# Attention: key copies, rotary exchange and score order

## The chip, the cores and the metric

The kernel runs on one core of a Trainium2 chip. The metric is device time in microseconds, the median of several executions.

## The reference

One inference step of a denoising trunk of four layers. A layer is a half-step SwiGLU feed-forward, a mixer, and a second such feed-forward, each with RMS norms around it and with shift, scale and gate from a conditioning vector; that makes twelve sub-layers. The mixers are attention (layers 0 and 3), a short convolution and a bidirectional gated scan. There are 128 prompt tokens and 256 sample tokens of 1024 features, in fp32. The attention has 16 query heads and 4 key/value heads of 64 features. For the sample tokens, queries and keys are rotated, and the keys are those of the band of 128 positions around the query and 128 cached ones; for the prompt tokens there is no rotation:

```python
def apply_rope(x, cos, sin):
    x1, x2 = jnp.split(x, 2, axis=-1)
    return jnp.concatenate([x1 * c - x2 * s, x1 * s + x2 * c], axis=-1)
s_lat = einsum(q, k_band) * ATTN_SCALE          # masked to the window
s_ctx = einsum(q, k_ctx) * ATTN_SCALE
p = softmax(concatenate([s_lat, s_ctx, sink]))
o = p_lat @ v_band + p_ctx @ v_ctx ;  return o.reshape(B, L, ATTN_DIM) @ w_o
```

The outputs are the tokens of both groups, the prompt's keys and values, and the scan's states.

## The kernel before, in words

All 384 tokens are kept together, features across the 128 partitions. Each weight block of 128 x 1024 comes by one load into one of four raw buffers; ScalarE rounds it to a high part (line 1925) and VectorE subtracts for the low part (line 2081), in a ring of six; three products of high and low parts make one product of TensorE (lines 1671 to 1673, 24 passes per block). There is no scheduler: each engine has its own list of work, written out by hand, and waits on semaphores. SyncE issues the loads in block order; load b waits until block b - 4 is split (`need(sp, w_lo_made, b - RAW + 1)`).

The attention is sub-layers 1 and 10. It has twelve projection blocks of 128 features, in the order of `QKV_CHUNKS`: two of keys, query 0, two of values, queries 1 to 7, and then eight blocks of the output weight. A query block holds two heads. Its parts:

- `take` (line 713, ScalarE) copies a projection out of PSUM. `dup` (line 568) is a product with a 0/1 matrix that puts one key head on both halves of the partitions; `copy_key` (line 728) takes it out to `kd`.
- `rotate` (line 580) is a product with a permutation that exchanges the 32-feature halves of the sample tokens of one key head or query block. GpSimd multiplies the original by the cosine (`cosine`, line 885), VectorE the exchanged one by the sine out of PSUM (line 803), and adds them (line 807). There are twelve rotations per attention, five of them ahead of the loop.
- `scores` (lines 595 to 603) are the products of a query block with keys and cached keys, `maxima` (line 819), `probs` (line 746) and `normalize` (lines 834 to 840) the softmax; `turn_probs` (line 614) transposes a head's probabilities, `values` (lines 632 to 639) multiplies them with the values, `output` (lines 753 and 754) copies the result and GpSimd's `low_part` (line 889) makes its low part.
- The loop has seven steps j. In each TensorE projects one block (step j: block 5 + j, query j + 1), transposes head 2j - 2, rotates the new query, does `values(j - 2)`, transposes head 2j - 1 and does `scores(j + 1)`. In step 0 it transposes the values and the prompt's keys instead (line 555).
- In sub-layer 1 alone a unit of the modulation is computed inside the attention, out of eight slabs of 512 KB (line 1792; `unit_half`, four slabs each), loaded by SyncE among the weights: three at b = 3, three at b = 6, two at b = 8 (`load_unit`).

Of the kernel before, what the change touches and what calls it, by code (L numbers as in the profile page):

```python
# [14 lines left out]
P = 128  # L15
D = 1024
# [29 lines left out]
def host_constants():  # L46
# [7 lines left out]
    rot = np.zeros((P, P), np.float32)  # L54
    rot[m ^ 32, m] = 1.0
    dup = np.zeros((P, 2, P), np.float32)
    duprot = np.zeros((P, 2, P), np.float32)
    for g in range(2):
        dup[64 * g + m % 64, g, m] = 1.0
        duprot[64 * g + ((m % 64) ^ 32), g, m] = 1.0  # L60
# [11 lines left out]
    attn = np.concatenate([rot, dup.reshape(P, -1), duprot.reshape(P, -1), cos, sin * sign,  # L72
                           band[:, 0].reshape(P, -1), np.zeros((P, P)), band[:, 1].reshape(P, -1)],
# [20 lines left out]
def build(nc, ins, outs, n_sub=12):  # L94
# [35 lines left out]
    QKV_CHUNKS = [DC, DC + 1, 0, DC + 2, DC + 3] + list(range(1, DC))  # L130
# [208 lines left out]

    def stores_until(s):  # L340

        return 2 * sub_kind[:s].count("attn")
# [33 lines left out]
    attn_k = place("attn_k", [P, 5 * P + 2 * TS + KEYS], F32, x_end - 2 * D * 4)  # L376
# [14 lines left out]
    rot_m = attn_k[:, 0:P]  # L391
    dup_m = [attn_k[:, P * (1 + g):P * (2 + g)] for g in range(2)]
    duprot_m = [attn_k[:, P * (3 + g):P * (4 + g)] for g in range(2)]
    cos_t = attn_k[:, 5 * P:5 * P + TS]
    sin_t = attn_k[:, 5 * P + TS:5 * P + 2 * TS]
    band_t = attn_k[:, 5 * P + 2 * TS:]
# [3 lines left out]
    rope_rot, k_dup_done, k_dup_copied = sem("rope_rot"), sem("k_dup_done"), sem("k_dup_copied")  # L400
# [118 lines left out]
    ROPE_ORDER = [("k", 0), ("k", 1), ("q", 0), ("k", 2), ("k", 3)] + [("q", j) for j in range(1, DC)]  # L519
    FIRST_ROPES = 5  # L520
    Q_AT = {j: ROPE_ORDER.index(("q", j)) for j in range(DC)}

    def qkv_bank(p):

        return p if p < 4 else 0 if p == 4 else 7

    def rope_bank(n):

        return 6 + n % 2 if n < FIRST_ROPES else 7

    def rope_dst(n):
        kind, i = ROPE_ORDER[n]
        return kd[:, i, TP:T] if kind == "k" else qkv[:, i, TP:T]

    def pe_attn(pe, s, first_two, in_block, out_part, ada_half, ada_turn):
        mm = nc.tensor.matmul
        a, mi, b0 = attn_number(s), mixer_number(s), first_block[s]
        taken = len(QKV_CHUNKS) * a
# [8 lines left out]
        def turn_values():  # L547

            pe.wait_ge(qkv_taken, taken + 5)
            pe.wait_ge(k_dup_copied, KVH * (a + 1))  # L550
            for n in range(NT + 1):
                for c in range(2):
                    src = qkv[:, DC + 2 + c, n * P:(n + 1) * P] if n < NT else qkv[:, DC + c, 0:P]
                    at = 2 * (n % 2) + c
                    last = nc.tensor.transpose(psum[4 + n // 2][:, at * P:(at + 1) * P], src, ident)
                if n % 2 == 1:
                    last.then_inc(attn_turned, 1)

        def dup(g):

            if g == 0:
                pe.wait_ge(qkv_taken, taken + 1)
            elif g == 1:
                pe.wait_ge(attn_turn_copied, 4 * a + 1)
            else:
                pe.wait_ge(qkv_taken, taken + 2)
                pe.wait_ge(k_dup_copied, KVH * a + g - 1)
            mm(psum[4 + (g + 1) % 2][:, 0:T], dup_m[g % 2], qkv[:, DC + g // 2, :], start=True,
               stop=True).then_inc(k_dup_done, 1)

        def rotate(n):
            kind, i = ROPE_ORDER[n]
            if n >= FIRST_ROPES:
                pe.wait_ge(qkv_taken, taken + n + 1)
            elif n >= 2:
                pe.wait_ge(rope_sin, ROPE * a + n - 1)
                if kind == "q":
                    pe.wait_ge(qkv_taken, taken + 3)
# [296 lines left out]
    def gp_attn(gp, s):  # L875
# [18 lines left out]
        for n in range(FIRST_ROPES):  # L894
            cosine(n)
# [1558 lines left out]
```

## Time and profile before

| | |
|---|---|
| time, median of 3 runs (lowest, highest) | 3026.55 us (3024.98, 3030.62) |
| profiled execution: span from the first to the last instruction | 3023.0 us |
| TensorE busy | 2968.9 us, 98% |
| VectorE, ScalarE, GpSimd busy | 73%, 38%, 20% |
| first attention, scores 0 to the first output product | 354.52 to 428.01 us |
| mean granted TensorE clock | 0.997 |

The profiled execution's own time is its span and what lies around it; no other time of it is kept, so it is set beside the median of the runs. The profile is one execution. Times in a timeline are microseconds from the start of the span. PE is TensorE, DVE VectorE, ACT ScalarE, POOL GpSimd, SPq SyncE's queue. A plain fp32 product shows as two passes. Durations of TensorE's passes overlap, so what a group holds is read from the start of its first pass to the start of the work behind it.

### The profile page before, as it was taken

The page shows a single profiled execution, that of the slowest core. Times are in us where ns is not written, and L with a number is a line of the kernel's source. Part 1 is how long each engine was busy: PE and PEld are TensorE (multiplying, and loading weights), DVE is VectorE, ACT ScalarE, POOL GpSimd, SP SyncE. Part 2 cuts the span into 40 slices and gives each one's busy share as a digit, 9 for nine tenths or more (in the row PEclk, how much of TensorE's full clock was granted, in tenths as well). Part 3 has the DMA queues.
Part 4 walks back from the last instruction along what each step waited for, and adds up shares of the span by engine and source line. Part 5 has one row for each costly group of instructions (what it writes and reads, how often), then busy time and mean ns, then how long its engine had stood idle before and what let it go on. Part 6 is the DMA issues. An engine that isn't in the chain of part 4 may idle for free.

```text
span 3023.0 us, 46915 instructions
## 1 busy us (share of the span) xinstructions
PE 2968.9 (98%) x18458; PEld 2750.8 (91%) x18458; DVE 2194.7 (73%) x2831; ACT 1152.8 (38%) x1966; POOL 594.5 (20%) x586
## 2 busy tenths in 40 slices
PE   7999999999999999999999999999999999999999
PEld 6999888999999998999899999979999999888998
DVE  6888678887877656888887576768887888775444
ACT  4222664223322424222422365553224222664222
POOL 1111212112211212112211144541122112211001
PEclk9999999999999999999999999999999999999999
DMA  8667435665665445766566443337675766333443
GB/s 303 208 212 215 138 86 190 209 209 168 212 210 172 117 134 166 222 211 197 181 209 202 133 117 95 103 96 230 209 215 166 222 211 197 110 79 119 126 127 96
DMA packets 565935, 515.61 MB, mean 171 GB/s; under 512 B 43013, under 2 KB 499286, under 8 KB 563926
## 3 DMA queue, kind: packets, MB, share of 16 engines
q1 hardware_dynamic: 565158, 512.37, 55.7%
q8 instruction: 148, 2.42, 0.3%
q14 instruction: 69, 0.57, 0.1%
q10 hardware_dynamic: 560, 0.25, 0.0%
HBM read 509.31 MB, written 3.24 MB: 170 GB/s over the span
## 4 chain that ended last, share of the span: by engine, by line
PE 91%; issue 3%; DVE 2%; ACT 1%; POOL 1%; DMA 1%; SPq 0%; DVEq 0%; POOLq 0%; ACTq 0%
PE bank L1671 19%; PE bank L1673 19%; PE bank L1672 19%; PE bank L1720 9%; PE bank L1722 9%; PE bank L1721 9%; PE bank L1688 2%; PE bank L1695 1%; PE bank L614 1%; PE bank L639 1%; PE bank L1753 1%; DMA ada_first<-w_ada 1%; POOL small L2358 0%; POOL small L2363 0%; ACT tmp L1978 0%
## 5 line engine op out<-in xcount | busy, mean ns | idle before, releaser
L1671 PE MATMUL bank<-h_hi,w_hi 128*128 128x384 f32 x3328 | 1120.7, 337 | 0.0
L1673 PE MATMUL bank<-h_hi,w_lo 128*128 128x384 f32 x3328 | 1115.1, 335 | 0.0
L1672 PE MATMUL bank<-h_lo,w_hi 128*128 128x384 f32 x3328 | 1114.0, 335 | 0.0
L1925 ACT ACTIVATE w_hi<-raw 128x1024 fp32r<-128x1024 f32 x646 | 680.5, 1061 | 1030.9 <-PE bank L1673 478.2
L2081 DVE TENSOR_TENSOR w_lo<-raw,w_hi 128x1024 fp32r<-128x1024 f32 x648 | 812.2, 1277 | 328.5 <-ACT w_hi L1925 323.6
L2108 DVE SCALAR_TENSOR_TENSOR fold<-ada_raw,cond,fold 128x1024 f32<-128x1024 f32 x462 | 638.7, 1439 | 0.1
L1671 PEld LDWEIGHTS bank<-h_hi,w_hi 128*128 128x128 f32 x3328 | 625.5, 188 | 10.9 <-ACT tmp L1944 1.6
L1672 PEld LDWEIGHTS bank<-h_lo,w_hi 128*128 128x128 f32 x3328 | 625.4, 188 | 6.1
L1673 PEld LDWEIGHTS bank<-h_hi,w_lo 128*128 128x128 f32 x3328 | 625.3, 188 | 0.0
L2399 POOL TENSOR_TENSOR h_lo<-tmp,h_hi 128x384 fp32r<-128x384 f32 x176 | 280.4, 1593 | 1737.6 <-DVE h_hi L2142 1737.6
L1720 PE MATMUL bank<-w_hi,h_hi 128*128 128x512 f32 x1056 | 415.4, 393 | 0.0
L1722 PE MATMUL bank<-w_hi,h_lo 128*128 128x512 f32 x1056 | 413.7, 392 | 0.0
L1721 PE MATMUL bank<-w_lo,h_hi 128*128 128x512 f32 x1056 | 413.2, 391 | 0.0
L1944 ACT ACTIVATE tmp<-bank 128x384 f32<-128x384 f32 x176 | 86.5, 491 | 481.4 <-PE bank L1673 479.1
L2138 DVE TENSOR_TENSOR tmp<-bank,tmp 128x384 f32<-128x384 f32 x176 | 97.9, 556 | 230.7 <-PE bank L1673 228.5
L1722 PEld LDWEIGHTS bank<-w_hi,h_lo 128*128 128x128 f32 x1056 | 198.2, 188 | 42.2
L1720 PEld LDWEIGHTS bank<-w_hi,h_hi 128*128 128x128 f32 x1056 | 198.3, 188 | 38.4
L1721 PEld LDWEIGHTS bank<-w_lo,h_hi 128*128 128x128 f32 x1056 | 198.3, 188 | 37.9
L2002 ACT ACTIVATE hf<-bank,mod,s_cols 128x128 f32<-128x128 f32 x288 | 106.5, 466 | 33.9 <-PE bank L1753 27.4
L2180 DVE TENSOR_TENSOR og<-bank,g_rows 128x512 f32<-128x512 f32 x72 | 49.3, 685 | 53.0 <-ACT tmp L1978 53.0
L1720 PE MATMUL bank<-w_hi,o_hi 128*128 128x512 f32 x192 | 77.1, 401 | 1.4 <-DVE tmp L942 1.0
L2115 DVE TRANSPOSE_TENSOR_REDUCE fold_sums<-fold 128x64 f32<-128x2048 f32 x33 | 76.0, 2304 | 0.0
(204 smaller groups left out, 2422.4 us busy)
## 6 DMA issues: line engine op xcount, KB each, us to landing
raw<-w_ffn_in SPq DMA_DIRECT2D x352, 512.0 KB, 5.0
ada_raw<-w_ada SPq DMA_DIRECT2D x264, 512.0 KB, 4.2
raw<-w_ffn_out SPq DMA_DIRECT2D x176, 512.0 KB, 4.6
raw<-w_hgrn_in SPq DMA_DIRECT2D x40, 512.0 KB, 4.0
g_rows<-g_dram SPq DMA_DIRECT2D x12, 1024.0 KB, 6.7
raw<-w_attn_qkv SPq DMA_DIRECT2D x24, 512.0 KB, 6.1
raw<-w_conv_in SPq DMA_DIRECT2D x24, 512.0 KB, 4.9
ada_first<-w_ada SPq DMA_DIRECT2D x16, 512.0 KB, 11.7
```

Of the source, the lines that this page charges most:

```text
L1671: mm(out, wh, h_hi[:, k, :], start=(k == 0), stop=False)
L1672: mm(out, wh, h_lo[:, k, :], start=False, stop=False)
L1673: last = mm(out, wl, h_hi[:, k, :], start=False, stop=(k == DC - 1))
L1720: mm(out, hi[:, tokens(t)], w_hi[:, b % RING, columns(n)], start=opens, stop=False)
L1721: mm(out, hi[:, tokens(t)], w_lo[:, b % RING, columns(n)], start=False, stop=False)
L1722: return mm(out, lo[:, tokens(t)], w_hi[:, b % RING, columns(n)], start=False, stop=closes)
L1925: A(w_hi[:, b % RING, :], raw[:, b % RAW, :], ACT.Copy).then_inc(w_hi_made, 1)
L2002: last = A(hf[:, t, k, :], psum[2 * t + half][:, k % 4 * P:(k % 4 + 1) * P], ACT.Identity, bias=mod[:, 3 * e * DC + k, g:g + 1], scale=s_c ...
L2081: V.tensor_tensor(w_lo[:, b % RING, :], raw[:, b % RAW, :], w_hi[:, b % RING, :].bitcast(F32), ALU.subtract).then_inc(w_lo_made, 1)
L2108: V.scalar_tensor_tensor(out=acc, in0=slab, scalar=c, in1=acc, op0=ALU.mult, op1=ALU.add).then_inc(fold_made, 1)
L2138: V.tensor_tensor(tmp[:, 2 + f % 2, :], psum[7][:, 0:T], tmp[:, f % 2, :], ALU.mult).then_inc(b_read, 1)
L2399: G.tensor_tensor(h2_lo[:, f % H2, :], tmp[:, 2 + f % 2, :], h2_hi[:, f % H2, :].bitcast(F32), ALU.subtract).then_inc(h2_lo_made, 1)
```

## The change

The products `dup` and `rotate` are gone, with their constant matrices. The two key projections are copied out of PSUM twice each, to both halves of the partitions, by ScalarE (first) and VectorE (second). The halves are exchanged by transfers within SBUF that SyncE issues, two for a key head and four for a query block, into four buffers; GpSimd then does both products and the sum. The last value block is projected last, so each query is projected a step earlier; its values are transposed in step 6. In steps 1 and 6 `scores(j + 1)` stand ahead of `values` and the second transpose. On SyncE the key exchanges 0, 1 and 3 stand ahead of load 8, exchange 5 ahead of load 13, the others behind a load (`KEY_SWAPS`, `QUERY_SWAPS`).

```diff
-    QKV_CHUNKS = [DC, DC + 1, 0, DC + 2, DC + 3] + list(range(1, DC))
+    QKV_CHUNKS = [DC, DC + 1, 0, DC + 2] + list(range(1, DC)) + [DC + 3]
...
-    attn_k = place("attn_k", [P, 5 * P + 2 * TS + KEYS], F32, x_end - 2 * D * 4)
+    attn_k = place("attn_k", [P, 2 * TS + KEYS], F32, x_end - 2 * D * 4)
...
+    rope_more = place("rope_more", [P, 2, TS], F32, x_end - 2 * TS * 4)
+    rope_of = [rope_tmp[:, 0, :], rope_tmp[:, 1, :], rope_more[:, 0, :], rope_more[:, 1, :]]
+    ROPE_BUFFERS = len(rope_of)
...
-    ROPE_ORDER = [("k", 0), ("k", 1), ("q", 0), ("k", 2), ("k", 3)] + [("q", j) for j in range(1, DC)]
-    FIRST_ROPES = 5
+    TAKES = len(QKV_CHUNKS) - 2
+    FIRST_BLOCKS = 5
+    ROPE_ORDER = [("k", 0), ("k", 1), ("q", 0), ("k", 2), ("q", 1), ("k", 3)] + [("q", j) for j in range(2, DC)]
+    FIRST_ROPES = 6
+    KEY_SWAPS, QUERY_SWAPS = {8: (0, 1, 3), 13: (5,)}, {8: 2, 13: 4} | {b: b - 8 for b in range(14, 20)}
...
+    def swap_runs(n):
+        if ROPE_ORDER[n][0] == "k":
+            return [(0, 32, 96), (96, 0, 32)]
+        return [(to, to ^ 32, 32) for to in range(0, P, 32)]
...
+    def copy_keys(copy, c):
+        rows = [slice(0, HD), slice(HD, P)]
+        copy(qkv[:, DC + c, 0:TP], psum[c][:, 0:TP])
+        for x in range(2):
+            for half in rows:
+                last = copy(kd[half, 2 * c + x, :], psum[c][rows[x], 0:T])
+        return last
...
-            pe.wait_ge(rope_sin, ROPE * a + FIRST_ROPES + j - (1 if j == 0 else 0))
-            in_block(b0 + FIRST_ROPES + j, 7)
+            pe.wait_ge(qkv_taken, taken + take_number(FIRST_BLOCKS + j - 1))
+            in_block(b0 + FIRST_BLOCKS + j, 7)
             if j == 0:
                 turn_values()
             else:
                 turn_probs(2 * j - 2)
-            rotate(FIRST_ROPES + j)
+            if j in (1, DC - 2):
+                if j == DC - 2:
+                    turn_last_values()
+                scores(j + 1)
             if j >= 2:
                 values(j - 2)
             if j >= 1:
                 turn_probs(2 * j - 1)
-            scores(j + 1)
+            if j not in (1, DC - 2):
+                scores(j + 1)
...
-        def cosine(n):
+        def rope(n):
+            gp.wait_ge(rope_swapped[n % ROPE_BUFFERS], swaps_made(a, n))
+            G.tensor_tensor(rope_of[n % ROPE_BUFFERS], rope_of[n % ROPE_BUFFERS], sin_t, ALU.mult).then_inc(rope_sin, 1)
+            G.tensor_tensor(rope_place(n), rope_place(n), cos_t, ALU.mult).then_inc(rope_cos, 1)
+            gp.wait_ge(rope_sin, ROPE * a + n + 1)
+            gp.wait_ge(rope_cos, ROPE * a + n + 1)
+            G.tensor_tensor(rope_place(n), rope_place(n), rope_of[n % ROPE_BUFFERS], ALU.add).then_inc(rope_add, 1)
...
+        def swap(s, n):
+            a, (kind, i) = attn_number(s), ROPE_ORDER[n]
+            if kind == "k":
+                sp.wait_ge(k_copied[i // 2], a + 1)
+            else:
+                sp.wait_ge(qkv_taken, TAKES * a + take_number(QKV_CHUNKS.index(i)))
+            need(sp, rope_add, ROPE * a + n + 1 - ROPE_BUFFERS)
+            for to, of, rows in swap_runs(n):
+                sp.dma_start(rope_of[n % ROPE_BUFFERS][to:to + rows, :], rope_place(n)[of:of + rows, :]
+                             ).then_inc(rope_swapped[n % ROPE_BUFFERS], 16)
...
             for b in range(n_blocks(s)):
+                if sub_kind[s] == "attn":
+                    for n in KEY_SWAPS.get(b, ()):
+                        swap(s, n)
                 if s > 0 or b >= 4:
                     load_block(b0 + b)
+                if sub_kind[s] == "attn" and b in QUERY_SWAPS:
+                    swap(s, QUERY_SWAPS[b])
```

## Rows read from the trace of the kernel before

**Rows 1.** Page, part 4: the chain that ended last, by engine.
```profile
PE 91%; issue 3%; DVE 2%; ACT 1%; POOL 1%; DMA 1%; SPq 0%; DVEq 0%; POOLq 0%; ACTq 0%
```

**Rows 2.** Windows, one loop step: us, busy by engine, clock, DMA share, GB/s.
```profile
372.36:382.35 9.99, 9.99 (x89) 9.03 (x88) 8.91 (x29) 7.58 (x23) 0.73 (x1) 1.00 0.18 54
```

**Rows 3.** Timeline, TensorE, first attention ahead of its loop: start, us, instruction.
```profile
336.76 0.81 PE L568 MATMUL bank<-qkv,attn_k 128*128 128x384 f32 x2
338.37 0.42 PE L1792 MATMUL bank<-unit_slab,cond 128*32 128x256 f32 x4
...
344.52 0.81 PE L568 MATMUL bank<-qkv,attn_k 128*128 128x384 f32 x2
346.77 1.93 PE L1792 MATMUL bank<-unit_slab,cond 128*32 128x256 f32 x32
...
353.27 0.89 PE L568 MATMUL bank<-qkv,attn_k 128*128 128x384 f32 x2
354.52 0.49 PE L595 MATMUL bank<-kd,qkv 64*128 64x256 f32 x2
```

**Rows 4.** Timeline, TensorE, first attention: in the loop.
```profile
361.41 0.60 PE L580 MATMUL bank<-qkv,attn_k 128*128 128x256 f32 x2
363.41 0.49 PE L595 MATMUL bank<-kd,qkv 64*128 64x256 f32 x2 [1.40 <-DVE qkv L807]
...
370.20 0.68 PE L580 MATMUL bank<-qkv,attn_k 128*128 128x256 f32 x2
371.48 0.30 PE L614 MATMUL bank<-base_k,pr 128*128 128x128 f32 x1 [0.60 <-ACT pt L737]
...
379.15 0.68 PE L580 MATMUL bank<-qkv,attn_k 128*128 128x256 f32 x2
379.76 0.33 PE L632 MATMUL bank<-pt,vt 128*64 128x128 f32 x2
```

**Rows 5.** Timeline, TensorE, second attention: before the loop.
```profile
2617.24 0.81 PE L568 MATMUL bank<-qkv,attn_k 128*128 128x384 f32 x2
2619.20 0.52 PE L1671 MATMUL bank<-h_hi,w_hi 128*128 128x384 f32 x1
...
2624.72 0.49 PE L595 MATMUL bank<-kd,qkv 64*128 64x256 f32 x2
```

**Rows 6.** Tile view, the unit's last slab: issue ns, when, landing.
```profile
L1572 SPq DMA_DIRECT2D unit_slab<-w_ada x1: 433/433/433, 340.7 to 340.7; - x1
DMA to landing us min/median/max: 4.9/4.9/4.9
```

**Rows 7.** Timeline, ScalarE: copy of query 0 in the first and second attention.
```profile
342.43 0.47 ACT L713 ACTIVATE qkv<-bank 128x384 f32<-128x384 f32 x1
...
2614.09 0.47 ACT L713 ACTIVATE qkv<-bank 128x384 f32<-128x384 f32 x1
```

**Rows 8.** Groups by line, GpSimd's cosine product: count, busy us, mean ns.
```profile
L885 POOL TENSOR_TENSOR qkv<-qkv,attn_k 128x256 f32<-128x256 f32 x16 | 11.7, 732 | 93.1 <-PE bank L580 93.1
```

**Rows 9.** DMA view, issues by line: KB each, median us to landing.
```profile
hg_in<-state_hgrn SPq DMA_DIRECT2D x8, 128.0 KB, 3.6
```

**Rows 10.** Waits of SyncE's queue, 280 to 440: total us, times, longest.
```profile
SPq L1582 <- DMA g_dram<-g_out: 8.4, 1, 8.4
```

**Rows 11.** Timeline, VectorE and GpSimd: two instructions that overlap.
```profile
382.93 1.00 DVE L834 TENSOR_TENSOR soft<-soft 128x3 f32<-128x3 f32 x1
...
382.91 1.00 POOL L889 TENSOR_TENSOR o_lo<-tmp,o_hi 128x384 fp32r<-128x384 f32 x1 [2.27 <-ACT o_hi L754]
```

**Rows 12.** Windows of 1 us, 324 to 328: first and last of four.
```profile
324.00:325.00 1.00, 1.00 (x6) 1.00 (x6) 0.53 (x2) 1.00 (x5) 1.00 (x2) 0.60 0.00 0
...
327.00:328.00 1.00, 1.00 (x8) 1.00 (x8) 1.00 (x2) 1.00 (x2) 1.00 (x1) 0.69 0.00 0
```

**Rows 13.** Timeline, VectorE: the weight split in step 0, first attention.
```profile
363.27 1.22 DVE L2081 TENSOR_TENSOR w_lo<-raw,w_hi 128x1024 fp32r<-128x1024 f32 x1
```

**Rows 14.** Page, part 5, ScalarE's weight split: count, busy us, mean ns.
```profile
L1925 ACT ACTIVATE w_hi<-raw 128x1024 fp32r<-128x1024 f32 x646 | 680.5, 1061 | 1030.9 <-PE bank L1673 478.2
```

More of the change, by code:

```diff
@@ L338, in build, with tokens @@
     out_stored = sem("out_stored")
+    def tokens(t):
+        return slice(t * P, (t + 1) * P)
     def stores_until(s):
@@ L537, in pe_attn @@
         a, mi, b0 = attn_number(s), mixer_number(s), first_block[s]
-        taken = len(QKV_CHUNKS) * a
+        taken = TAKES * a
         def turn_cache():
@@ L547, in turn_values @@
         def turn_values():
[L549 to L578, printed above, removed]
-            stat, src = (duprot_m[i % 2], DC + i // 2) if kind == "k" else (rot_m, i)
-            mm(psum[rope_bank(n)][:, 0:TS], stat, qkv[:, src, TP:T], start=True, stop=True).then_inc(rope_rot, 1)
+            pe.wait_ge(qkv_taken, taken + take_number(3))
@@ new lines, in turn_values, with turn_last_values @@
+            for c in range(2):
+                pe.wait_ge(k_copied[c], a + 1)
+            pe.wait_ge(attn_turn_copied, 4 * a + 1)
+            for n in range(NT):
+                nc.tensor.transpose(psum[5][:, tokens(n)], qkv[:, DC + 2, tokens(n)], ident)
+            for c in range(2):
+                last = nc.tensor.transpose(psum[4][:, c * P:(c + 1) * P], qkv[:, DC + c, 0:TP], ident)
+            last.then_inc(attn_turned, 1)
+        def turn_last_values():
+            pe.wait_ge(qkv_taken, taken + TAKES)
+            for n in range(NT):
+                last = nc.tensor.transpose(psum[7][:, tokens(n)], qkv[:, DC + 3, tokens(n)], ident)
+            last.then_inc(attn_turned, 1)
@@ L582, in scores @@
         def scores(j):
             g = 2 * j // (HEADS // KVH)
-            pe.wait_ge(rope_add, ROPE * a + Q_AT[j] + 1)
-            pe.wait_ge(k_dup_copied, KVH * a + g + 1)
+            pe.wait_ge(rope_add, ROPE * a + max(ROPE_AT["q", j], ROPE_AT["k", g]) + 1)
             if j == 0:
-                pe.wait_ge(qkv_taken, taken + 5)
+                for c in range(2):
+                    pe.wait_ge(k_copied[c], a + 1)
+                pe.wait_ge(qkv_taken, taken + take_number(3))
             else:
@@ L648, in unit_half @@
             if half == 0:
-                pe.wait_ge(qkv_taken, taken + 2)
+                pe.wait_ge(k_copied[1], a + 1)
             else:
@@ L657, in pe_attn @@
         turn_cache()
-        dup(0)
-        pe.wait_ge(qkv_taken, taken + 1)
-        rotate(0)
-        rotate(1)
         for u in units:
@@ L774, in act_attn @@
             probs(2 * j)
-            take(FIRST_ROPES + j)
+            take(FIRST_BLOCKS + j)
             if j == 0:
@@ L779, in act_attn @@
                 copy_probs(2 * j - 2)
+            if j == DC - 2:
+                copy_last_values()
             probs(2 * j + 1)
@@ L1525, in group_of @@
         return 0 if t == 0 else 1
-    def tokens(t):
-        return slice(t * P, (t + 1) * P)
     def square_number(e, t, n, of_y):
```

92 lines of the change are left out of this document (28 added, 64 removed).

## The prediction

> **What bounds the kernel now.** First the chain of waits: TensorE holds 91% of it, so a microsecond taken from TensorE's own queue is a microsecond of the time, unless something else then comes late [rows 1]. Then busy time by stretch: in a middle step of the attention loop TensorE is busy for 9.99 of 9.99 us, VectorE for 8.91, ScalarE for 7.58, GpSimd for 0.73 [rows 2]. VectorE is the next limit, and GpSimd has room. Then TensorE's timeline, for what the rotary products cost where they stand [rows 3 to 5]. Other sub-layers aren't touched.
>
> The sum is made against the profiled execution: its span is 3023.0 us, and the median of the runs shown, 3026.55, lies 3.55 above it. I add that again at the end.
>
> **What goes.** Per attention, four products that double the keys and twelve that exchange halves.
> - Ahead of the loop, in the first attention: from the first product to the next other work 1.61, 2.25 and 1.25 us, 5.11 in all [rows 3]. In the second the middle group takes 1.96 for 2.25 [rows 5]; with the others in that ratio it is 4.45.
> - In the loop: step 0, the product and the wait for the rotated query, 363.41 - 361.41 = 2.00. Step 1, the product and 0.60 of waiting for ScalarE, 371.48 - 370.20 = 1.28. Steps 2 to 6, 379.76 - 379.15 = 0.61 each, 3.05. Together 6.33 [rows 4].
> - The transposes are eight as before; three of them (some 0.33 us) go from step 0 to step 6.
> The ceiling is 5.11 + 4.45 + 2 x 6.33 = 22.2 us. On VectorE, two rotary instructions per step go; at step 0 they held 363.27 - 361.41 = 1.86 us with their waits [rows 13].
>
> **What comes, at its price.** A query's exchange is four issues on SyncE, one after the other. I take 0.43 each, from a slab's issue [rows 6]: the last starts 1.3 us after the first, and SyncE is held 1.7. No transfer within SBUF and none of 32 KB is in this trace. The nearest row for the landing is a state of 128 KB, 3.6 us [rows 9]. Below, it can't be less than the issue, 0.43; above, the strided 8 KB write of gains held SyncE for 8.4 [rows 10]. I take 3.6. The Trainium skill, DMA: Bandwidth & Descriptors, "Anatomy of one DMA", puts the fixed part at about 2.0 us (fitted on GpSimd's path); by it the sum would gain some 4 us more, and no row here shows it.
>
> A rotation is three GpSimd instructions of 128x256 where there was one of 0.73 [rows 8]: 2.3 us with the wait between them. Six stand ahead of the loop, one behind the other, 14 us. In the loop they stand ahead of the subtraction that makes the low part, one per step: 2.3 + 1.0 us in a step of 9.4, and ScalarE's output needs only the subtraction of two chunks before, so I cost this at nothing; were it late, ScalarE's copies would be by the same amount.
>
> The keys' copies, five on ScalarE and five on VectorE at up to 0.5 each [rows 7], lie beside TensorE's third and fourth projection: nothing. Without that cover 2.5 us once. VectorE's part also holds SyncE: the third key's exchange waits for it, and weight load 8 behind that. The smaller constants land before the stage and save nothing.
>
> **First attention.** The new wait that matters is query 0's exchange on SyncE, ahead of the last two slabs of the modulation unit. It waits for ScalarE's copy, which ends at 342.43 + 0.47 = 342.90 because it stands behind a split [rows 7]. Four issues later, at 344.6 and 345.0, come the slabs; the second was issued at 340.7 and landed 4.9 later [rows 6]. So it lands at 349.9, and with the last quarter of the unit's product (0.48) TensorE goes on at 350.4. Before, that product ended at 346.77 + 1.93 = 348.70 [rows 3]. The first two of the three groups are thus lost, and 1.7 us more. The third group's 1.25 is saved, but it covered VectorE's addition to the modulation, of which I estimate 0.35 exposed (it lies between 0 and 1.25). Scores 0 start at 354.52 + 1.7 - 0.9 = 355.3: 0.8 late.
> - Scores 1: they followed scores 0 by 363.41 - 354.52 = 8.89 [rows 3, 4]; less 2.00 and 0.33, TensorE is ready at 355.3 + 6.56 = 361.9. Query 1's projection runs some 4.3 us from 350.4, its copy ends at about 355.2; last issue 356.5, landing 360.1, rotated 362.4. Gain there: 363.4 - 362.4 = 1.0.
> - Scores 2, now ahead of a transpose: the exchange stands behind load 14, which waits for VectorE's split. That ended at 363.27 + 1.22 = 364.49, 9.97 after scores 0 began [rows 3, 13]; without the rotary part 8.1, so at 363.4. Load 0.4, last issue 1.3, landing 3.6, rotation 2.3: 371.0. TensorE is ready 370.20 - 363.41 = 6.79 after scores 1 [rows 4], at 369.2, and waits for 1.8. Scores and transpose have only changed places, and the first of the two began at 371.48 [rows 4]: gain 0.5.
> - Steps 2 to 6: the same chain takes 8.1 + 7.6 = 15.7 us from one scores to the next but one, and two steps of 9.99 - 0.61 = 9.4 leave 3 to spare; scores 7, moved up, have some 0.5. So 3.05 - 0.33 = 2.7 more.
> Net gain 3.2.
>
> **Second attention.** No unit here. Query 0's copy ends at 2614.09 + 0.47 = 2614.56 [rows 7]; last issue 2615.9, landing 2619.5, rotated 2621.8. TensorE would be ready at 2624.72 - 4.45 = 2620.3 [rows 5]: gain at scores 0 only 2.9. Load 9, now behind that exchange, is issued at 2616.3 and lands about 2620.3 (4.0, my estimate from the 3.6 and an issue); with both splits, 1.06 and 1.22 [rows 13, 14], load 13 can go at 2622.6, and behind it query 1's exchange: rotated at 2622.6 + 7.6 = 2630.2, where TensorE is ready at 2621.8 + 6.56 = 2628.4. Scores 2 by the chain: 2621.8 + 15.7 = 2637.5 (ready 2637.0). Its place before, at the first attention's distances, was 2624.72 + 371.48 - 354.52 = 2641.7: gain 4.2. With 2.7 for the steps: 6.9.
>
> Sum: 3.2 + 6.9 = 10.1 us. 3023.0 - 10.1 + 3.55 = 3016.5. Of the ceiling, 12 us come back as late exchanges.
>
> **The rivals.**
> - *All rotations in time* (the exchange lands almost with its issue): all waits but the slabs' go. First attention -0.8 + 6.33, second 4.45 + 6.33, together 16.3: 3010.2. For it: 32 KB is little. Against it: 128 KB took 3.6.
> - *GpSimd holds VectorE up, and VectorE becomes the bound.* A 128x3 addition of VectorE that started at 382.93 took 1.00 us, as long as GpSimd's 128x384 subtraction, started at 382.91 [rows 11]. If every rotation does that, VectorE has 8.91 - 0.85 + 2.2 = 10.3 per step against TensorE's 9.4; ten steps lose 0.9 each, 9 us of the 10: 3025.6. It decides once over 1.3 of a rotation's 2.2 us fall on such VectorE instructions; against it, the three maxima of each head read PSUM. The Trainium skill, SBUF — State Buffer, "Who interferes with whom", says so of any VectorE instruction with two SBUF inputs beside a GpSimd one that reads SBUF: the later one blocks fully. The rows agree.
> - *Late exchanges, slower.* If an exchange lands like the gains' write, 8.4 us, the chain from split to rotated query is 21.2 us, more than two steps, and the loop runs at 10.6 a step where it was 10.0. With the first waits 4.8 longer the first attention loses some 8 and the second 8: 3042. It decides from a landing of about 5.4. For it: only those 8.4 us. Against it: that write goes to HBM in elements, this one moves rows of 1 KB.
> - *Clock.* TensorE will stand still for some 5 us between 343 and 350. After a smaller stop the granted clock fell to 0.60 from 324 and was back in the fourth slice, 0.69 [rows 12]; such a fall costs half of some 3.5 us, 1.7: 3018.2. It is inside the forecast's own range.
> - *The products don't bound* (TensorE's queue waits elsewhere for all that is freed): nothing changes. Rows 1 and 2 speak against it.
>
> **How the numbers follow.** The forecast has 0.52, all in time 0.18, VectorE bound 0.20, late exchanges 0.07, no effect 0.03. No change means within 0.2%, 6 us, which is about what a measurement can tell here. Forecast and all in time count as faster, and 0.04 of VectorE bound: 0.74. Same: 0.13 of VectorE bound, 0.01 of the late ones, 0.03: 0.17. The rest, 0.09, is slower. The range from 3007 to 3025 takes in all in time with the clock's 1.7 and more, and nearly all of VectorE bound; what it leaves out is the late exchanges.
>
> **What would show it.** Right: no product with the constants on TensorE; a stop of TensorE until about 349.9 on the slabs in the first attention; scores 0 about 0.8 later there and 2.9 earlier in the second; waits of 0.5 to 2 us for GpSimd's addition before scores 1 and 2; middle steps of 9.4. An exchange that lands in under 2 us, or waits for GpSimd in the middle steps, would refute the sizes; VectorE splits much over 1.2 us with TensorE waiting for a normalised head would show the lock. Wrong altogether: middle steps of 10 or more.

## The result: slower by 0.4%

The changed kernel took 3038.77 us (median of 5 runs, 3035.39 to 3043.78), the kernel before 3026.55 beside it: a ratio of 1.0039, 95% interval 1.0029 to 1.005. The forecast was 3016.5 and its range ended at 3025; sign and size were both wrong. The profiled execution of the changed kernel, 3043.78 us with a span of 3042.0, was the slowest of the five; that of before, with a span of 3023.0, lies at the fast end of its runs. So the traces differ by 19.0 us and the medians by 12.2.

TensorE's share of the chain of waits fell, and every other engine's grew [rows 1]:
```profile
PE 86%; issue 4%; DVE 4%; DMA 2%; ACT 2%; POOL 2%; SPq 1%; another core or an unknown queue 0%; DVEq 0%; POOLq 0%; ACTq 0%
```

The middle step of the loop did what was foretold. Window of one step: us, then busy time (and count) of TensorE, its weight loads, VectorE, ScalarE and GpSimd, granted clock, DMA share, GB/s [rows 2]:
```profile
400.62:410.07 9.45, 9.45 (x87) 8.70 (x86) 8.88 (x27) 7.29 (x23) 3.12 (x4) 1.00 0.24 72
```
A step takes 9.45 us instead of 9.99, and TensorE is never idle. But VectorE is still busy for 8.88 (8.91 before), though two of its instructions went.

The time went where TensorE stops. Its timeline in the first attention (start, us, instruction, and in brackets the idle time before it with what ended it) [rows 3, 4]:
```profile
347.04 1.28 PE L1785 MATMUL bank<-unit_slab,cond 128*32 128x256 f32 x16 [4.41 <-ACT ada_rows L1925]
351.21 1.08 PE L1785 MATMUL bank<-unit_slab,cond 128*32 128x256 f32 x8 [2.90 <-DMA unit_slab<-w_ada]
352.57 1.08 PE L1785 MATMUL bank<-unit_slab,cond 128*32 128x256 f32 x8 [0.28 <-DMA unit_slab<-w_ada]
...
360.66 0.70 PE L598 MATMUL bank<-kd,qkv 64*128 64x256 f32 x4 [0.27 <-DVE mod L2115]
...
379.07 1.23 PE L598 MATMUL bank<-kd,qkv 64*128 64x256 f32 x4 [4.81 <-POOL qkv L864]
...
433.88 0.80 PE L598 MATMUL bank<-kd,qkv 64*128 64x256 f32 x2 [7.06 <-POOL qkv L864]
...
2643.11 0.70 PE L598 MATMUL bank<-kd,qkv 64*128 64x256 f32 x4 [2.59 <-issue]
2653.14 0.70 PE L598 MATMUL bank<-kd,qkv 64*128 64x256 f32 x4 [3.30 <-POOL qkv L864]
...
2706.99 0.70 PE L598 MATMUL bank<-kd,qkv 64*128 64x256 f32 x4 [1.06 <-POOL qkv L864]
```
The last three rows are of the second attention [rows 5]. Scores 0 start at 360.66 (354.52 before), scores 2 stop for 4.81 us and scores 7 for 7.06: the two that were moved up in their steps. From the first product of the key projection to the first product of the output, the first attention takes 122.40 us (104.06 before), the second 96.15 (97.64 before). So the first is 18.3 us longer and the second 1.5 shorter; 2 us more lie outside, where 27.0 us were at the lower clock instead of 18.0.

In the first attention the stops over 0.25 us add up to 22.6 us (2.5 before), 20.1 more. The removed products take off 9.4 (the ceiling of 5.11 + 6.33 without its 2.00 of waiting). That makes 10.7 of the 18.3. Of the other 7.6, slow products explain some 6.3, as an estimate: TensorE worked for 15.9 us at the lower clock (3.4 before), and half of the difference counts as lost. The last 1.3 stay open. Windows of 7 us, same columns as above [rows 12]:
```profile
347.00:354.00 7.00, 3.79 (x33) 1.24 (x34) 1.09 (x1) 0.36 (x1) 6.57 (x10) 0.55 0.90 265
354.00:361.00 7.00, 6.73 (x32) 6.62 (x33) 1.82 (x3) 1.97 (x3) 0.69 (x1) 0.71 1.00 291
...
434.00:441.00 7.00, 7.00 (x55) 6.17 (x55) 0.00 (x0) 0.71 (x2) 0.77 (x1) 0.58 0.02 1
```
At the three long stops of this attention the granted clock falls to its lower level, 1.2 GHz: for 10.2 us from 347.8, for 10.2 from 429.7 (4.2 of them still in the stop), and for 3.4 from 378.5, 23.9 us in this attention where before had 3.4.

Who was late is read from SyncE's issues [rows 6]:
```profile
334.81 3.55 SPq L1572 DMA_DIRECT2D rope_tmp<-kd  x4
...
339.69 0.59 SPq L1530 DMA_DIRECT2D raw<-w_attn_qkv  x1
344.64 2.42 SPq L1572 DMA_DIRECT2D rope_more<-qkv  x4
347.10 1.06 SPq L1548 DMA_DIRECT2D unit_slab<-w_ada  x2
...
370.27 0.33 SPq L1530 DMA_DIRECT2D raw<-w_attn_o  x1
370.70 2.41 SPq L1572 DMA_DIRECT2D rope_more<-qkv  x4
...
420.21 0.34 SPq L1530 DMA_DIRECT2D raw<-w_attn_o  x1
420.65 2.41 SPq L1572 DMA_DIRECT2D rope_more<-qkv  x4
423.10 0.58 SPq L1553 DMA_DIRECT2D g_dram<-g_out  x1
```
and ScalarE's copies of queries 0, 2 and 7 [rows 7]:
```profile
344.13 0.49 ACT L708 ACTIVATE qkv<-bank 128x384 f32<-128x384 f32 x1
...
366.87 0.49 ACT L708 ACTIVATE qkv<-bank 128x384 f32<-128x384 f32 x1 [0.69 <-PE bank L1666]
...
416.27 0.49 ACT L708 ACTIVATE qkv<-bank 128x384 f32<-128x384 f32 x1 [0.67 <-PE bank L1666]
```
Query 2 is in SBUF at 367.36 and its exchange is issued at 370.70; query 7 at 416.76 and 420.65. Both stand behind a weight load, and the load behind VectorE's split. VectorE's timeline shows why that split is not earlier than before [rows 13]:
```profile
366.94 1.64 DVE L822 TENSOR_SCALAR pr<-pr,soft 128x384 f32<-128x384 f32 x3
368.50 1.75 DVE L2074 TENSOR_TENSOR w_lo<-raw,w_hi 128x1024 fp32r<-128x1024 f32 x1
...
416.57 2.48 DVE L822 TENSOR_SCALAR pr<-pr,soft 128x384 f32<-128x384 f32 x3
418.97 1.21 DVE L2074 TENSOR_TENSOR w_lo<-raw,w_hi 128x1024 fp32r<-128x1024 f32 x1
...
420.97 0.95 DVE L822 TENSOR_SCALAR pr<-pr,soft 128x384 f32<-128x384 f32 x3
```
Three normalising passes take 0.95 us alone and 2.48 beside GpSimd's rotation and low part (415.58 to 418.83). The split of step 0 ends at 370.25, 9.6 us after scores 0; before it was 9.97. From query 2 on, each 32 KB issue of an exchange landed 2.4 to 3.7 us later [rows 9], but for the last one of query 7 in the first attention, which took 9.0. The keys' issues, with weights and slabs in flight, took 1.8 to 7.2 us.

### The profile page after: what moved, and what is told of

Same layout as the page of the kernel before. It is cut to its first block, busy times and chain, and to the rows that moved or that the text cites. A ratio compares the mean times of both kernels' runs of the same rounds, so it can differ in the third digit from the quotient of the medians.

```text
span 3042.0 us, 46885 instructions
## 1 busy us (share of the span) xinstructions
PE 2961.4 (97%) x18394; PEld 2747.0 (90%) x18394; DVE 2190.8 (72%) x2793; ACT 1152.1 (38%) x1964; POOL 634.9 (21%) x634
## 4 chain that ended last, share of the span: by engine, by line
PE 86%; issue 4%; DVE 4%; DMA 2%; ACT 2%; POOL 2%; SPq 1%; another core or an unknown queue 0%; DVEq 0%; POOLq 0%; ACTq 0%
PE bank L1664 18%; PE bank L1666 18%; PE bank L1665 18%; PE bank L1713 9%; PE bank L1715 9%; PE bank L1714 8%; PE bank L1681 2%; PE bank L1688 1%; DVE pr L822 1%; DMA raw<-w_attn_qkv 1%; DVE sm L801 1%; PE bank L1746 1%; DMA ada_first<-w_ada 1%; ACT pr L739 1%; DMA rope_more<-qkv 0%
```

## Experiments

Theory A: the exchanges are late, by their place in SyncE's queue, and the clock falls behind the stops. Theory B: GpSimd's operations hold VectorE up. Theory C: the moved scores ask too early. Each run was timed against the kernel before in the same session (medians 3024.95 to 3026.55). The spans of the attentions are measured as above; "half" is the time at 1.2 GHz in the first.

| kernel | median us | ratio [95%] | first attention | half | second |
|---|---|---|---|---|---|
| before | 3026.55 | 1 | 104.1 | 3.4 | 97.6 |
| changed | 3038.77 | 1.0039 [1.0029, 1.0050] | 122.4 | 23.9 | 96.2 |
| no_rotation | 3013.50 | 0.9960 [0.9946, 0.9975] | 97.9 | 0 | 89.5 |
| lock_only | 3018.29 | 0.9976 [0.9967, 0.9986] | 101.2 | 0 | 93.7 |
| no_exchange | 3019.42 | 0.9985 [0.9975, 0.9994] | 102.2 | 3.4 | 93.8 |
| no_move | 3031.80 | 1.0021 [1.0011, 1.0030] | 111.5 | 13.7 | 97.0 |
| unit_first | 3033.09 | 1.0032 [1.0018, 1.0046] | 108.1 | 13.7 | 100.9 |
| gains_later | 3034.45 | 1.0033 [1.0020, 1.0046] | 114.6 | 17.1 | 96.0 |
| query_ahead | 3025.46 | 1.0000 [0.9990, 1.0009] | 107.1 | 10.2 | 94.1 |
| ahead_no_move | 3029.65 | 1.0008 [0.9998, 1.0017] | 107.1 | 10.2 | 94.7 |
| ahead_unit | 3021.75 | 0.9987 [0.9978, 0.9997] | 103.0 | 3.4 | 94.7 |
| act_swap | 3022.26 | 0.9988 [0.9978, 0.9997] | 104.2 | 8.7 | 93.4 |
| ahead_unit_keys | 3020.50 | 0.9983 [0.9974, 0.9993] | 101.6 | 3.4 | 94.1 |

**no_rotation: what the products were worth.** No exchange is issued, GpSimd does nothing for it, and the scores wait so:
```diff
-            pe.wait_ge(rope_add, ROPE * a + max(ROPE_AT["q", j], ROPE_AT["k", g]) + 1)
+            pe.wait_ge(qkv_taken, taken + take_number(QKV_CHUNKS.index(j)))
...
```


> The rotation is left out of this kernel (no exchange, no GpSimd products and sum; the scores wait only for the takes of the queries and keys by ScalarE). It shows what the removed TensorE work is worth when nothing is put in its place. Theory A (the exchange by DMA comes late and stops TensorE, and the granted clock falls behind the stops): both attentions keep what TensorE no longer does, so 16 to 20 us faster than before, near 3008; the first attention's stretch from the first key product to the first output product falls from 122.4 us to about 93 to 96, and the normalise passes of VectorE go back from 530 ns to about 410 with GpSimd silent. Theory B (the products were not what bound the attention; the softmax on VectorE does): within 5 us of before, 3021 to 3027, with TensorE stopping in the steps for VectorE.

Measured 0.40% under before, 12 us where 16 to 20 were expected, and 6.2 + 8.2 = 14.4 by the trace. So the products did bound the attention, but the ceiling of 22.2 was never to be had: from scores 6 to the first output product it takes 17.1 us (15.76 before), since the softmax of the last two heads ends the loop. And 2.7 us of stop stay ahead of the unit's second half, where TensorE waits for ScalarE's copy of the unit's rows; before, the second group of removed products (2.25 us) stood there. One step, in the columns of the windows, and VectorE's rows of step 0, whose split ends at 360.16, 8.0 us after scores 0:
```profile
385.77:395.23 9.46, 9.46 (x88) 8.71 (x87) 7.99 (x26) 7.31 (x23) 1.18 (x1) 1.00 0.19 58
...
358.08 0.95 DVE L822 TENSOR_SCALAR pr<-pr,soft 128x384 f32<-128x384 f32 x3
358.94 1.22 DVE L2065 TENSOR_TENSOR w_lo<-raw,w_hi 128x1024 fp32r<-128x1024 f32 x1
```

**no_exchange: GpSimd's work without the DMAs.**
```diff
-            gp.wait_ge(rope_swapped[n % ROPE_BUFFERS], swaps_made(a, n))
-            G.tensor_tensor(rope_of[n % ROPE_BUFFERS], rope_of[n % ROPE_BUFFERS], sin_t, ALU.mult).then_inc(rope_sin, 1)
+            kind, i = ROPE_ORDER[n]
+            if kind == "k":
+                gp.wait_ge(k_copied[i // 2], a + 1)
+            else:
+                gp.wait_ge(qkv_taken, TAKES * a + take_number(QKV_CHUNKS.index(i)))
+            G.tensor_tensor(rope_of[n % ROPE_BUFFERS], rope_place(n), sin_t, ALU.mult).then_inc(rope_sin, 1)
...
-                    for n in KEY_SWAPS.get(b, ()):
-                        swap(s, n)
...
-                    swap(s, QUERY_SWAPS[b])
...
```


> Only the exchange of the halves by DMA is left out: GpSimd does the same cosine product, sine product and sum in the same order, the sine product on the halves as they stand, as soon as the copy by ScalarE is there. Theory A (late exchanges): most of what the kernel without any rotation gains comes back, 3010 to 3017; the stops of 4.8 us ahead of scores 2 and 7.1 us ahead of scores 7 in the first attention go, and no stretch of 10 us at half the clock is left there. Theory B (the products of GpSimd hold VectorE up through the port they share): still at 3028 to 3038, since all the work of GpSimd is still there; normalise passes stay near 530 ns, and TensorE goes on stopping for VectorE.

Measured 3019.42, a little above theory A's 3010 to 3017. Leaving out the exchange alone takes off more than the whole loss: theory A's main part. But 0.25% still separates it from no_rotation, in which GpSimd's operations are gone too, and a middle step takes 9.61 us:
```profile
388.63:398.24 9.61, 9.51 (x87) 8.72 (x86) 9.05 (x27) 7.06 (x22) 3.50 (x5) 1.00 0.20 55
```

**lock_only: GpSimd works, nobody waits for it.** As no_exchange, but all results go to spare buffers and the scores wait as in no_rotation.


> GpSimd does all its products and sums, as many and as large as in the changed kernel, but into spare buffers, and nothing waits for them; there is no exchange, and the scores use queries and keys that are not rotated (the rotation is left out). It parts the two ways in which GpSimd's work can cost. The kernel without the exchange took 4.3 us more in each attention than the one without any rotation (102.2 against 97.9, 93.8 against 89.5), 0.25% of the time. Theory B (GpSimd holds VectorE's passes up while it runs): the same 4 us stay although nobody waits, steps of 9.6 us, 0.10 to 0.20% below before (3020 to 3023). Latency (the scores wait for the 2.3 us chain): the cost goes, steps of 9.45, 0.35 to 0.45% below before (3012 to 3015).

Measured 0.9976, between the ranges of the two readings: theory B's part is 0.16% of the 0.25%. The intervals of neighbouring runs overlap, so the split rests on the traces, where it is 3.3 of 4.3 us in the first attention and 4.2 of 4.3 in the second. The step takes 9.61 us, as in no_exchange, with VectorE at 9.05:
```profile
387.65:397.26 9.61, 9.49 (x88) 8.71 (x87) 9.05 (x27) 7.06 (x22) 3.51 (x5) 1.00 0.18 55
```
and VectorE's and GpSimd's timelines show the overlap:
```profile
395.48 1.97 DVE L822 TENSOR_SCALAR pr<-pr,soft 128x384 f32<-128x384 f32 x3
397.38 1.75 DVE L2073 TENSOR_TENSOR w_lo<-raw,w_hi 128x1024 fp32r<-128x1024 f32 x1
...
395.49 0.74 POOL L864 TENSOR_TENSOR rope_tmp<-qkv,attn_k 128x256 f32<-128x256 f32 x1 [5.12 <-ACT qkv L708]
```
The step is then paced by VectorE: ScalarE waits for its maxima, 2.6 us in this step.

**no_move: the scores back at the ends of their steps.**
```diff
-            if j in (1, DC - 2):
-                if j == DC - 2:
-                    turn_last_values()
-                scores(j + 1)
+            if j == DC - 2:
+                turn_last_values()
...
-            if j not in (1, DC - 2):
-                scores(j + 1)
+            scores(j + 1)
```


> One part undone: scores 2 and scores 7 go back to the end of their steps (1 and 6), behind the outputs, where the other scores stand. Theory C (the moved scores ask for their query before its rotation is ready): the stops ahead of scores 2 (4.8 us) and scores 7 (7.1 us) of the first attention go or fall under 2 us, the half-clock stretch of 10.2 us ahead of the output goes too, and the time is 3026 to 3032, 7 to 12 us below the changed kernel. Theory A in its plain form (the rotation is late wherever the scores stand): the exchange of query 7 landed 9.0 us after its issue, so the stop only moves behind the values' products of the step; 2 to 5 us saved at the most, 3034 to 3037.

Measured 1.0021, about 5 us off the change's loss. The stop at scores 7 falls from 7.06 to 2.32, not under 2, and the one at scores 2 gives way to 2.46 us of waiting at a transpose:
```profile
427.79 0.70 PE L598 MATMUL bank<-kd,qkv 64*128 64x256 f32 x4 [2.32 <-POOL qkv L861]
```
Theory C holds, as something that makes A worse. The last exchange landed nearly as late here (8.4 us).

**unit_first: keys 0, 1, 2 and query 0 exchanged behind load 8 and the slabs.**
```diff
-                if sub_kind[s] == "attn":
+                if sub_kind[s] == "attn" and b != 8:
                     for n in KEY_SWAPS.get(b, ()):
...
-                if sub_kind[s] == "attn" and b in QUERY_SWAPS:
+                if sub_kind[s] == "attn" and b in QUERY_SWAPS and b != 8:
                     swap(s, QUERY_SWAPS[b])
...
                         load_unit(s, u, b)
+                    if b == 8:
+                        for n in (0, 1, 3, 2):
+                            swap(s, n)
```


> One order changed: the exchanges of keys 0, 1, 3 and of query 0 go behind weight load 8 and behind the part of the gains' weights that is issued with it, instead of ahead of them. If the queue on SyncE is what delays the gains' weights (theory A, first half): the stops at 351 to 353 us (2.9 and 0.3 us) and the one of 4.4 us ahead of them shrink to what before had (under 1.5 us together), the half-clock stretch of 10.2 us in the first attention is shorter, and 4 to 8 us are saved against the changed kernel, 3031 to 3035; scores 0 may wait 1 to 2 us longer for the later exchange, which would eat part of it. If it is not the queue (the weights are late for another reason, the bandwidth of the DMA engines): no gain, 3037 to 3042.

So the queue did delay the slabs: the stops on them went, and 14 us of the first attention. But 7 of these were at scores 7, whose exchange landed in time here, and of the 4.41 us ahead of the unit's second half 2.34 stay (under 1.5 was expected), about as in no_rotation (2.67). The second attention paid: scores 0 wait there for 4.88 us (2.59 in the changed kernel). The median is in the range expected, but 1.0032 can't be told from the changed kernel's 1.0039. TensorE's timeline, first and second attention:
```profile
346.45 3.21 PE L1788 MATMUL bank<-unit_slab,cond 128*32 128x256 f32 x32 [2.34 <-ACT ada_rows L1928]
...
2630.01 0.83 PE L598 MATMUL bank<-kd,qkv 64*128 64x256 f32 x4 [4.88 <-issue]
```

**query_ahead: from load 13 on, a query's exchange ahead of the load.**
```diff
+                if sub_kind[s] == "attn" and b >= 13:
+                    swap(s, QUERY_SWAPS[b])
                 if s > 0 or b >= 4:
                     load_block(b0 + b)
-                if sub_kind[s] == "attn" and b in QUERY_SWAPS:
+                if sub_kind[s] == "attn" and b == 8:
                     swap(s, QUERY_SWAPS[b])
```


> One order changed: from weight load 13 on, the exchange of a query stands on SyncE ahead of the load of its block instead of behind it. In the changed kernel the copy of query 2 was done at 367.4 us and its exchange issued at 370.7, that of query 7 at 416.3 and 420.7, because the load between waited for VectorE's split. If that queueing is what made the rotations late (theory A): the exchanges go 3.4 to 4.4 us earlier, the stop of 4.8 us ahead of scores 2 falls to about 1.4, the one of 7.1 us ahead of scores 7 to under 0.5, in the second attention the 3.3 us ahead of scores 1 to about 1.4, the half-clock stretches at 378 and 430 us go, and the kernel comes to 0.0 to 0.2% above before (3025 to 3031). If the transfers themselves or the GpSimd products are late whatever the place in the queue: unchanged, 0.35 to 0.45% above before.

The whole loss went: 1.0000. Query 7, in ScalarE's and SyncE's rows and at its scores:
```profile
410.70 0.49 ACT L708 ACTIVATE qkv<-bank 128x384 f32<-128x384 f32 x1 [0.84 <-PE bank L1668]
...
411.22 2.41 SPq L1572 DMA_DIRECT2D rope_more<-qkv  x4
413.67 0.58 SPq L1530 DMA_DIRECT2D raw<-w_attn_o  x1
...
421.31 0.70 PE L598 MATMUL bank<-kd,qkv 64*128 64x256 f32 x4
```
Issued 0.03 us after its copy, with no stop left at scores 7; at scores 2 there is one of 0.88 us, for VectorE. The load behind it goes out 0.9 us after its split, and no stop follows from that. So the order on SyncE made the loop's loss: theory A. It did so twice. The wait for the split goes, and the transfer itself is shorter: from query 2 on an issue landed after a median of 1.8 us here and 3.0 behind a load. In the changed kernel the first rows of query 2's exchange moved 2.5 us after its issue, when the packets of the load ahead (371.2 to 373.5) were nearly through; here 1.2 us after.

Of the 7.06 us at scores 7 some 5.9 were the late landing (9.0 instead of about 3.1), which did not come again here. Whether that alone would explain the gain is asked in the next run.

**gains_later: the gains' write behind those of the new keys and values.**
```diff
-            if sub_kind[s] != "ffn":
+            if sub_kind[s] not in ("ffn", "attn"):
                 write_gains(s)
             if sub_kind[s] == "attn":
                 sp_core(sp, s)
+                write_gains(s)
```


> One transfer moved: the write of the gains (8 KB in elements of 4 bytes, 2048 of them), which SyncE issues 0.04 us behind the last exchange of query 7, goes behind the writes of the new keys and values. In the changed kernel the last two issues of that exchange landed 9.0 us after their issue, although their last packets were moved within 2 to 3 us. If the small elements hold back the exchange's completion: it lands within 4 us of its last issue, the stop ahead of scores 7 in the first attention falls from 7.1 us to under 2, and 5 to 10 us of the first attention come back (0.1 to 0.25% above before). If it was the load of code on the same DMA engine, or chance: the late landing is there again whenever that load falls on the exchange, and the time stays 0.3 to 0.45% above before.

By the trace of the changed kernel only the last of the four issues landed late. Here all landed within 3.6 us, and GpSimd began at 428.33 instead of 431.55, in steps that ran 2 us later:
```profile
428.33 0.72 POOL L860 TENSOR_TENSOR rope_more<-rope_more,attn_k 128x256 f32<-128x256 f32 x1 [7.32 <-DMA rope_more<-qkv]
```
The stop at scores 7 is 2.71, not under 2. Over four traces the exchange of query 7 took at most 9.0 (changed) and 8.4 us (no_move) where a code load of 16 KB fell on its last rows and the write of 4-byte elements stood behind it, 3.6 with the code load and no write (here), 3.3 with the write and the code load later (unit_first). So in these four it took both; one trace of each kind is no proof. The first attention is 7.8 us shorter, but the median, 1.0033, can't be told from 1.0039 and lies in the range of the other reading. So a landing in time, with the exchange still behind its load, gives back little, and query_ahead's gain is, as far as medians tell, that of the order. How often write and code load meet in unprofiled runs stays open.

**act_swap: ScalarE exchanges, in four copies of 32 rows.**
```diff
+            for to in range(0, P, 32):
+                last = A(rope_of[n % ROPE_BUFFERS][to:to + 32, :], rope_place(n)[to ^ 32:(to ^ 32) + 32, :], ACT.Copy)
+            last.then_inc(rope_swapped[0], 1)
...
+            if j < DC - 2:
+                exchange(6 + j)
...
```


> The exchange is made by ScalarE: four copies of 32 rows each in place of the DMAs, for keys and queries alike, in the gap after its split of a weight block; GpSimd's three operations stay. By the 0.49 us of a 64x384 copy an exchange takes 1.4 to 2.0 us. Theory A: no stop for a rotation is left in either attention, the stretch ahead of scores 0 is that of the kernel without an exchange, and the time lies between that kernel and before, 0.0 to 0.15% under before (3020 to 3025). Rival: ScalarE, busy 7.3 of 9.45 us in a step, gets 1.4 to 2.0 us more and its exponentials and copies come late in a chain that VectorE fills to 8.9 us: steps of 9.7 to 10.5 us instead of 9.45, 0.05 to 0.35% above before (3026 to 3036).

An exchange takes 1.70 us and the steps stay at 9.46, with ScalarE at 8.97 of them: the rival is refuted.
```profile
393.07:402.53 9.46, 9.46 (x88) 8.71 (x87) 8.80 (x27) 8.97 (x27) 3.14 (x4) 1.00 0.17 55
```
Theory A's range was right (0.9988), not its other signs: scores 2 still stop for a rotation (0.79 us in the first attention, 2.07 in the second), and in the first the exchanges of query 0 and key 2, 1.69 us each, hold ScalarE ahead of the unit's rows, and TensorE stops there for 6.54 us.

**ahead_unit: query_ahead, and the last slabs ahead of query 0's exchange.** At block 8, the exchange of query 0 goes behind the issue of the slabs.


> Two orders changed: the query exchanges ahead of their loads as in the run above, and in the part ahead of scores 0 the exchange of query 0 behind the last two slabs of the gains' weights (load 8 stays behind the keys' exchanges). Theory A: the slabs, which landed up to 352.5 us in the changed kernel, go 2.4 us earlier; the stops of 2.9 and 0.3 us there fall to about 0.5 while scores 0, which then had 0.3 us to spare, waits at most 1 us longer: 1 to 4 us less than the run above in the first attention, 0 to 1 us more in the second, where no slab is loaded: 0.1% below to 0.15% above before (3022 to 3029). If scores 0 is bound by the chain of GpSimd operations on keys 0 and 1 and not by the exchange, the same; if by the exchange of query 0, no gain over the run above.

Measured 0.9987, with an interval that ends at 0.9997: a little faster than before. In the first attention the stops on the slabs are gone, scores 0 wait for 0.27 us as in the changed kernel, and the time at the lower clock is 3.4 us instead of 10.2; it is 4.1 us shorter than in query_ahead. The second attention is 0.6 us longer.

**ahead_no_move: query_ahead with the scores back at the ends.** The diffs of query_ahead and no_move together.


> Query exchanges ahead of their loads, and scores 2 and 7 back at the ends of their steps. It asks what the moved scores are worth once the exchanges are in time. With late exchanges, undoing the move gained 0.18%. If the move only hurt because the exchanges were late (theory C joined to A): here undoing it costs 1 to 4 us against the kernel with exchanges ahead and scores moved, because in that one the scores found their queries ready and VectorE got its maxima earlier: 0.03 to 0.15% above before (3027 to 3030). If the move is bad in itself: 1 to 4 us faster than that kernel, 0.03 to 0.15% below before (3021 to 3025).

Measured 1.0008 against 1.0000. That is in the first reading's range, but the intervals overlap, and the attentions differ by 0.0 and 0.6 us. With exchanges in time the moved scores neither hurt nor earn anything that can be measured.

**ahead_unit_keys: besides ahead_unit, only key 0 exchanged ahead of load 8.**
```diff
-    KEY_SWAPS, QUERY_SWAPS = {8: (0, 1, 3), 13: (5,)}, {8: 2, 13: 4} | {b: b - 8 for b in range(14, 20)}
+    KEY_SWAPS, QUERY_SWAPS = {8: (0,), 13: (5,)}, {8: 2, 13: 4} | {b: b - 8 for b in range(14, 20)}
...
+                    if b == 8:
+                        swap(s, 1)
+                        swap(s, 3)
                     for u in range(*units_of[s]):
                         load_unit(s, u, b)
+                    if b == 8:
+                        swap(s, 2)
```


> The version with query exchanges ahead of their loads and the gains' slabs ahead of the exchange of query 0, and in addition only the exchange of key 0 ahead of weight load 8; those of keys 1 and 2 behind it. In the version before this one TensorE still stops 4.0 us ahead of the second half of the gains' product, against 2.4 in the kernel without an exchange, because the keys' exchanges hold load 8. If so, the stop falls to about 2.5 us and the first attention gains 1 to 2 us: 0.13 to 0.20% below before. In the second attention key 1 lands behind load 8; if that is over 3 us later than now (its product started 3.4 us behind key 0's), scores 0 wait longer and the gain is lost: 0.05 to 0.13% below before. Both lie within 3020 to 3025.

The stop is 2.93 us instead of 4.00, the first attention 1.4 us shorter than in ahead_unit, and the second 0.6. SyncE's issues (load 8 at 336.44, 339.69 in the changed kernel), and TensorE behind them:
```profile
334.58 1.81 SPq L1572 DMA_DIRECT2D rope_tmp<-kd  x2
336.44 1.09 SPq L1530 DMA_DIRECT2D raw<-w_attn_qkv  x1
...
342.45 1.05 SPq L1548 DMA_DIRECT2D unit_slab<-w_ada  x2
...
345.53 3.40 PE L1790 MATMUL bank<-unit_slab,cond 128*32 128x256 f32 x32 [2.93 <-ACT ada_rows L1930]
```
At 0.9983 it is the fastest version that does the whole change, under before and under the changed kernel; the intervals don't part it from ahead_unit and act_swap.

## Why the prediction was wrong

- **What the products are worth** was oversized: 22.2 us as a ceiling, 14.4 in the trace with nothing in their place. Part of the removed time is not gained, because the softmax ends the loop, and because the second group of products had covered a wait for ScalarE.
- **The step that failed: the chain from VectorE's split by the load to the moved scores.** "That ended ... 9.97 after scores 0 began; without the rotary part 8.1, so at 363.4." In no_rotation it does end 8.0 after scores 0, but in the changed kernel 9.6. GpSimd's rotation takes back 1.5 of the 1.9 us freed: beside it the addition of step 0 takes 0.48 us instead of 0.16, the normalising passes 1.64 instead of 0.95, the split 1.75 instead of 1.22. The split lets load 14 go, and the exchange stands behind the load. From scores 0 the chain to scores 2 was then 9.6 us to the split's end, 0.45 to the first issue, 1.8 to the last (SyncE held for 2.41, not 1.7), 3.1 to its landing and 3.4 for the rotation (its sum took 1.79 us): 18.4 us, where I had 15.7 with the landing at 3.6. So the landing, left open from 0.43 to 8.4, was the one term that came out shorter. Scores 2 came at 379.07 instead of 371.0: 5.4 of these 8.1 us from scores 0, 2.7 from the chain. The issue's 0.6 us could have been read: "none of 32 KB is in this trace" is wrong, the trace of before has one on SyncE:
```profile
4.50 0.62 SPq L1638 DMA_DIRECT2D vin<-hgrn_lb  x1
```
- **"Scores 7, moved up, have some 0.5" to spare** hung on the same chain. In the second attention they lacked 1.06 us; in the first the late landing, in no row of before, made it 7.06. I priced the wait behind the load, but did not ask whether the exchange had to stand behind it: query_ahead shows that this order is worth the whole loss against before (1.0039 to 1.0000). What query_ahead leaves in the first attention (107.1 us, 104.1 before) is the slabs' wait, which ahead_unit takes away.
- **Scores 0 in the first attention: 6.1 late, not 0.8.** The slabs went out at 347.10 instead of 344.6 (query 0's copy 1.7 later than taken, behind load 7, and the exchange's issues 0.7 longer), and the clock's fall cost more than the 1.7 us of the rival: 10.2 us at 1.2 GHz, 7.1 of them busy, some 3.5 lost by the same estimate. Load 7 goes out 2.0 later (334.33 for 332.38) because the issues of the three slabs ahead of it hold SyncE for 3.35 us instead of 1.53. They do so in no_rotation too (3.63) but not in ahead_unit (1.57), so it is not the exchange; why it varies is open.
- **Second attention:** scores 0 gained 2.1 (forecast 2.9), scores 1 gained 0.9 (forecast 3.4), the first output product 1.5 instead of 6.9. Scores 0 did not wait for query 0's exchange, which landed at 2639.20, but for GpSimd, which had two keys to rotate ahead of it. The prediction has the rotations "one behind the other", but put only the query's on the path. Three in a row took 8.9 us instead of 3 x 2.3, since products that started beside a split of VectorE took 1.82 and 1.70:
```profile
2634.13 0.74 POOL L860 TENSOR_TENSOR rope_tmp<-rope_tmp,attn_k 128x256 f32<-128x256 f32 x1 [7.04 <-DMA rope_tmp<-kd]
2634.83 1.82 POOL L861 TENSOR_TENSOR kd<-kd,attn_k 128x256 f32<-128x256 f32 x1
...
2639.76 1.70 POOL L860 TENSOR_TENSOR rope_more<-rope_more,attn_k 128x256 f32<-128x256 f32 x1
...
2642.29 0.72 POOL L864 TENSOR_TENSOR qkv<-qkv,rope_more 128x256 f32<-128x256 f32 x1
```
- **Right:** the products gone, middle steps of 9.4, and the stop on the slabs. **Half right:** waits for GpSimd's addition, which came at scores 2 in the first attention (4.81 us) and at scores 1 in the second (3.30), not at both in each and not at 0.5 to 2; and the keys' exchanges as something that holds load 8, which was named and priced at nothing (1.4 us of the first attention by ahead_unit_keys).
- **The rivals.** Late exchanges, with 0.07, came nearest to the time (3042), by luck: by the queue, and by a landing of that size only once. Its own chain of 21.2 us is 20.5 by the prediction's terms (15.7 with 8.4 for 3.6). GpSimd on VectorE got the mechanism, at 0.16% (5 us) by lock_only, and not the size: VectorE needs 8.9 to 9.05 us of a step, not 10.3. The Trainium skill, SBUF — State Buffer, "Who interferes with whom", counts multiplications by a column among the operations that can take the shared ports; I had read it for operations with two SBUF inputs alone, and the passes that were held longest are of the first kind (0.95 to 2.48 us). The two rivals were weighed one by one; what happened was both in a row, the lock delaying the split and the split the exchange.

## What to carry to other kernels

A transfer that is issued in order behind another inherits that one's wait: put the one whose data is ready first ahead, and check each pair for which of the two is really free to go. A short transfer issued behind a long load also waits for the load's packets (3.0 us to land instead of 1.8). Time freed on VectorE counts only after GpSimd's new work is laid over it (1.5 of 1.9 us went back). And a long stop of TensorE cost more than its length here: behind the one for the slabs, 7.1 us of work ran at 1.2 GHz.

## What the runs showed that was not expected

- 32 KB from SBUF to SBUF landed 1.8 us after issue with no load just ahead (query_ahead), and 2.4 to 3.7 behind one. Each issue held SyncE for 0.5 to 0.6 us; four of them cost more queue time than one load of 512 KB in the same loop (0.33).
- GpSimd is held as well: its 128x256 product that started at 346.97, 0.23 us behind a VectorE split of 1.35 us, took 1.71 us, where 0.72 is seen alone. The same section of the Trainium skill says that issue order decides which of the two blocks; the trace agrees: that product ran 0.6 us on after the split had ended.
- A small exchange's completion came 8.4 and 9.0 us after its last issue where a code load and a write of 4-byte elements met on it (two traces), though its last row began to move 3.1 and 3.0 us after that issue (two rows stood behind the code load).
- In no_exchange, with rotations at the earliest time, a middle step took 9.61 us; in the changed kernel, with late ones, 9.45. So what a rotation costs depends on which VectorE instructions it falls on, and an earlier one was dearer here.
